# A gather-and-combine expert stage: unrolled, V rows combined in four column groups, accumulator over 128 tokens

## The reference

```python
eid = ...                                   # (C, 128) chosen experts
g = jax.nn.softmax(top_s, axis=-1)...       # (C, 128) gate
u = expert_u[eid]
act = jax.nn.gelu(jnp.einsum('cd,ced->ce', xc, u).astype(jnp.float32))
return jnp.einsum('ce,ced->cd', (g * act).astype(xc.dtype), expert_v[eid])
```

## Time and profile before

| | us |
|---|---|
| median of three runs | 4412.84 |
| span of the profiled execution, first to last instruction (the profile gives no time around it) | 4247.4 |
| PE busy | 3836.9 (90%) |
| DVE busy | 2282.6 (54%) |
| POOL busy | 2122.0 (50%) |
| combine matmuls (L1564), busy | 2040.8 |
| dots (L1762), busy | 1286.0 |
| gathers on POOL, V (L1435) and U (L1426), busy | 1014.6 and 1005.5 |

### The profile page before, as it was taken

The page is one execution under the profiler, slowest core; times in us unless marked ns, Lnnn a source line. Parts: engine busy times, 40 slices in busy tenths (PEclk is TensorE's granted clock), DMA queues, the critical chain, the costliest instruction groups (busy, mean ns, idle before and its releaser), DMA issues.

```text
span 4247.4 us, 40209 instructions
## 1 busy us (share of the span) xinstructions
PE 3836.9 (90%) x10602; PEld 1129.1 (27%) x10602; DVE 2282.6 (54%) x5355; ACT 571.9 (13%) x879; POOL 2122.0 (50%) x2205
## 2 busy tenths in 40 slices
PE   7999998887499999999989989998898999899998
PEld 4444553343122122112212211221121122112111
DVE  2351552242857447655754764575467557546751
ACT  2331552232000001000100100000010000000000
POOL 0000000024356765765666567566657756765674
PEclk9998879998599999999999999999999999999999
DMA  2111006345499999999999999999999999999997
GB/s 69 30 45 42 0 0 193 104 137 175 187 323 366 396 351 327 395 394 323 371 388 360 321 394 390 321 358 384 365 318 385 396 336 350 396 373 318 380 403 259
DMA packets 362556, 1212.93 MB, mean 286 GB/s; under 512 B 42058, under 2 KB 66634, under 8 KB 358748
## 3 DMA queue, kind: packets, MB, share of 16 engines
q0 software_dynamic: 304128, 1107.43, 69.6%
q1 hardware_dynamic: 58204, 102.95, 7.7%
HBM read 1185.97 MB, written 24.26 MB: 285 GB/s over the span
## 4 chain that ended last, share of the span: by engine, by line
PE 33%; issue 16%; DMA 13%; POOL 10%; DVE 4%; ACT 1%; POOLq 0%; DVEq 0%; SPq 0%; ACTq 0%
PE y_acc L1564 21%; DMA v_rows<-expert_v,idx_v 12%; PE qp L1520 6%; POOL v_rows L1435 6%; PE xb L1554 4%; POOL u_rows L1426 4%; DVE x_out L1777 1%; PE tp_r L1541 1%; DMA u_rows<-expert_u,idx_u 0%; PE tp_r L1536 0%; DVE y_out L1783 0%; ACT y_out L1624 0%; DVE u_rows L1762 0%; DMA wq<-w_query 0%; POOLq L1424 0%
## 5 line engine op out<-in xcount | busy, mean ns | idle before, releaser
L1564 PE MATMUL y_acc<-v_rows,w_diag 128*32 128x512 f32 x4224 | 2040.8, 607 | 165.8 <-DMA v_rows<-expert_v,idx_v 63.4
L1762 DVE CUSTOM_DVE_ANT_0 u_rows<-u_rows,xb 128x1024 f32<-128x1024 f32 x1056 | 1286.0, 1220 | 1074.2 <-PE xb L1554 1053.3
L1435 POOL DMA_INDIRECT v_rows<-expert_v,idx_v x1056 | 1014.6, 961 | 707.1 <-PE y_acc L1564 432.2
L1426 POOL DMA_INDIRECT u_rows<-expert_u,idx_u x1056 | 1005.5, 952 | 466.4 <-issue 323.7
L1564 PEld LDWEIGHTS y_acc<-v_rows,w_diag 128*32 128x32 f32 x4224 | 381.7, 110 | 1355.9 <-issue 939.1
L1554 PE MATMUL xb<-parts,pick 96*128 96x512 bf16 x2112 | 654.1, 392 | 60.3 <-DVE dots L1762 37.7
L1554 PEld LDWEIGHTS xb<-parts,pick 96*128 96x128 bf16 x2112 | 147.5, 98 | 833.9 <-DVE dots L1762 593.1
L1520 PE MATMUL qp<-wq,xt 128*128 128x512 f32 x576 | 323.7, 653 | 0.5 <-DMA wq<-w_query 0.5
L352 PE MATMUL zp<-xT,w 128*128 128x512 f32 x512 | 251.4, 619 | 6.1 <-DMA w<-w_in 6.1
L1619 ACT ACTIVATE acts<-dots 128x32 f32<-128x32 f32 x33 | 7.6, 229 | 1662.0 <-DVE dots L1762 1662.0
L1520 PEld LDWEIGHTS qp<-wq,xt 128*128 128x128 f32 x576 | 90.4, 193 | 238.4 <-issue 238.4
(11 more groups left out here) (272 smaller groups left out, 2665.4 us busy)
## 6 DMA issues: line engine op xcount, KB each, us to landing
u_rows<-expert_u,idx_u POOLq DMA_INDIRECT x1056, 6.8
v_rows<-expert_v,idx_v POOLq DMA_INDIRECT x1056, 6.6
w<-w_in SPq DMA_DIRECT2D x16, 512.0 KB, 3.8
xT<-cache_k SPq DMA_DIRECT2D x8, 1024.0 KB, 5.4
xT<-cache_v SPq DMA_DIRECT2D x8, 1024.0 KB, 5.5
wq<-w_query SPq DMA_DIRECT2D x4, 2048.0 KB, 18.5
parts<-x_parts SPq DMA_DIRECT2D x99, 64.0 KB, 6.0
ko<-cache_k SPq DMA_DIRECT2D x8, 768.0 KB, 8.0
```

The lines of the kernel that those rows point to most:

```text
L1426: nc.gpsimd.indirect_dma_start(u_rows[:, t % U_SLOTS, :], None, expert_u, bass.IndirectOffsetOnAxis(ap=idx_u[par][:, t:t + 1], axis=0)).th ...
L1435: nc.gpsimd.indirect_dma_start(v_rows[:, t % V_SLOTS, :], None, expert_v, bass.IndirectOffsetOnAxis(ap=idx_v[par][:, t:t + 1], axis=0)).th ...
L1564: last = nc.tensor.matmul(acc[:, half], w_diag[:, par, t, :], v_rows[:, t % V_SLOTS, half], start=(t == 0), stop=(t == TB - 1))
L1762: nc.vector.tensor_tensor_reduce(out=u_rows[:, t % U_SLOTS, :], in0=u_rows[:, t % U_SLOTS, :], in1=xb[:, t % XB_SLOTS, :], scale=1.0, scal ...
```

## The change

It does six things in `expert_stage`; all else stays.

1. The loops over tiles go: each engine's program is written out over all 33 blocks, with waits against constants.
2. Gathers read their indices straight from idxT; the index copies go. POOL waits for a tile's routing (`kept`) itself.
3. `combine` takes two tokens at a time. Token t adds into column group t mod 4 of the array, that is into partitions 32 g to 32 g + 31 of `acc`; the two tokens' matmuls alternate by half. It waits for both V rows, and frees both slots at its end.
4. `acc` holds 128 tokens. The stationary operand is a window of 32 columns into a zeroed buffer that holds each weight in a place of its own (column 24 + 32 t + t // 4); the window's place decides the row. `weigh` is one strided product.
5. `finish`, `norm`, `store` and `load_resid` come once per tile, on 128 partitions (four transfers of every fourth row each), no longer once per block. The store of a tile is issued behind the second block of the next tile.
6. 6 U slots and 8 V slots, from 8 and 4.

The core of the diff:

```diff
-U_SLOTS = 8
-V_SLOTS = 4
+U_SLOTS = 6
+V_SLOTS = 8
+GROUPS_PE = 4
+EDGE = 24
...
-        w_diag = sb("w_diag", [P, 2, TB, TB])
+        w_diag = sb("w_diag", [P, 2, (TB + 1) * TB])
...
-            with pool.Fori(0, PT) as tile:
-                for j in range(QB):
-                    for t in range(TB):
-                        gather_u(QB * tile + j + 1, t, (j + 1) % 2)
-                        gather_v(QB * tile + j, t, j % 2)
+            for s in range(NTOK + TB):
+                if s < NTOK:
+                    gather_u(s)
+                if s >= TB:
+                    gather_v(s - TB)
...
+            for b in range(NB):
+                r, j = divmod(b, QB)
...
                 sp.wait_ge(dot_done, TB * (b + 1))
+                if b + 2 < NB:
+                    load_parts(b + 2)
+                if (j == 1 and r > 0) or b == NB - 1:
+                    store(r - 1)
+                    load_resid(r)
...
+            def combine(s):
+                b, t = divmod(s, TB)
+                r, j = divmod(b, QB)
+                end = QB - 1 if r < PT else 0
                 if t == 0:
                     pe.wait_ge(w_ready, b + 1)
-                    pe.wait_ge(acc_read, b + 1)
-                pe.wait_ge(v_landed[t % V_SLOTS], 16 * (V_USES * b + t // V_SLOTS + 1))
+                    if j == 0 and r > 0:
+                        pe.wait_ge(acc_read, r)
+                for s2 in (s, s + 1):
+                    pe.wait_ge(v_landed[s2 % V_SLOTS], 16 * (s2 // V_SLOTS + 1))
                 for half in HALVES:
-                    last = nc.tensor.matmul(acc[:, half], w_diag[:, par, t, :], v_rows[:, t % V_SLOTS, half],
-                                            start=(t == 0), stop=(t == TB - 1))
-                last.then_inc(v_free, 1)
+                    for t2 in (t, t + 1):
+                        g, col = t2 % GROUPS_PE, TB * t2 + EDGE - TB // GROUPS_PE * j
+                        last = nc.tensor.matmul(acc[TB * g:TB * (g + 1), half], w_diag[:, b % 2, col:col + TB],
+                                                v_rows[:, (TB * b + t2) % V_SLOTS, half],
+                                                start=(j == 0 and t2 < GROUPS_PE),
+                                                stop=(j == end and t2 >= TB - GROUPS_PE))
+                last.then_inc(v_free, 2)
...
+            for s in range(0, NTOK, 2):
+                for s2 in (s + TB, s + TB + 1):
+                    if s2 < NTOK:
+                        broadcast(s2)
+                combine(s)
+                for s2 in (s, s + 1):
+                    route(s2 // P + 1, s2 % P)
...
+                if b >= 2:
+                    dve.wait_ge(v_free, TB * (b - 1))
+                nc.vector.tensor_tensor(diagonal(b), by_group(acts[:]), by_group(gateT[:, b * TB:(b + 1) * TB]),
                                         ALU.mult).then_inc(w_ready, 1)
...
+            for b in range(NB):
+                r, j = divmod(b, QB)
+                for t in range(TB):
+                    if b + 1 < NB:
+                        dot(TB * (b + 1) + t)
+                    route(r + 1, TB * j + t)
+                if b + 1 < NB:
+                    if (b + 1) % QB == 0:
+                        dve.wait_ge(kept, (b + 1) // QB + 1)
+                    weigh(b + 1)
+                if j == QB - 1 or b == NB - 1:
+                    finish(r)
```

More of the change, by code:

```diff
@@ L1318 @@
 QB = P // TB
-U_SLOTS = 8
-V_SLOTS = 4
+NB = NTOK // TB
+U_SLOTS = 6
+V_SLOTS = 8
 XB_SLOTS = 2
@@ L1480, in _ @@
             load_tokens(1)
-            def block_done(b, j, rows):
-                sp.wait_ge(dot_done, TB * (b + 1))
[L1484 to L1499, removed]
+            for b in range(NB):
+                r, j = divmod(b, QB)
+                if j == 2 and r + 2 <= PT:
+                    sp.wait_ge(xt_used, r + 2)
+                    load_tokens(r + 2)
+                sp.wait_ge(dot_done, TB * (b + 1))
+                if b + 2 < NB:
[3 more added lines that the diff above has]
+                    load_resid(r)
+            store(PT)
+            sp.wait_ge(out_landed, 16 * GROUPS_PE * (PT + 1))
         @block.tensor
@@ L1546, in route, with broadcast @@
                     nc.tensor.transpose(tp[:, 1, :], number[:, 2, :], c.ident[:]).then_inc(turned, 1)
-            def broadcast(b, t, par, loads):
+            def broadcast(s):
+                b, t = divmod(s, TB)
                 if t == 0:
-                    pe.wait_ge(parts_landed[par], 48 * loads)
-                if not isinstance(b, int) or TB * b + t >= XB_SLOTS:
-                    pe.wait_ge(dot_done, TB * b + t - XB_SLOTS + 1)
+                    pe.wait_ge(parts_landed[b % 2], 48 * (b // 2 + 1))
+                if s >= XB_SLOTS:
+                    pe.wait_ge(dot_done, s - XB_SLOTS + 1)
@@ L1553, in broadcast @@
                 for half in HALVES:
-                    last = nc.tensor.matmul(xb[:, t % XB_SLOTS, half], pick[:, t, :], parts[:, par, half],
+                    last = nc.tensor.matmul(xb[:, s % XB_SLOTS, half], pick[:, t, :], parts[:, b % 2, half],
                                             start=True, stop=True)
                 last.then_inc(xb_ready, 1)
-            def combine(b, t, par):
+            def combine(s):
+                b, t = divmod(s, TB)
+                r, j = divmod(b, QB)
+                end = QB - 1 if r < PT else 0
@@ L1572, in _ @@
                 route(0, i)
-            pe.wait_ge(const_ready, 6)
-            for t in range(TB):
-                broadcast(0, t, 0, 1)
-            with pe.Fori(0, PT) as tile:
-                for j in range(QB):
-                    b = QB * tile + j
-                    for t in range(TB):
-                        broadcast(b + 1, t, (j + 1) % 2, 2 * tile + (j + 1) // 2 + 1)
-                        combine(b, t, j % 2)
-                        route(tile + 1, TB * j + t)
-            for t in range(TB):
-                combine(NB - 1, t, 0)
+            pe.wait_ge(const_ready, 5)
+            for s in range(0, TB, 2):
+                broadcast(s)
+                broadcast(s + 1)
+            for s in range(0, NTOK, 2):
[5 more added lines that the diff above has]
+                    route(s2 // P + 1, s2 % P)
         @block.scalar
@@ L1633, in _ @@
             gelu(0)
-            with act.Fori(0, PT) as tile:
-                for j in range(QB):
-                    for t in range(TB):
-                        route(tile + 1, TB * j + t)
-                    gelu(QB * tile + j + 1)
-                    norm(QB * tile + j)
-            norm(NB - 1)
+            for b in range(NB):
[3 more added lines that the diff above has]
+                if b + 1 < NB:
+                    gelu(b + 1)
+                if j == QB - 1 or b == NB - 1:
+                    norm(r)
         @block.vector
@@ L1759, in dot @@
[L1759 to L1761 removed]
+            def dot(s):
+                t = s % TB
+                dve.wait_ge(u_landed[s % U_SLOTS], 16 * (s // U_SLOTS + 1))
+                dve.wait_ge(xb_ready, s + 1)
                 nc.vector.tensor_tensor_reduce(
[L1763 removed]
+                    out=u_rows[:, s % U_SLOTS, :], in0=u_rows[:, s % U_SLOTS, :], in1=xb[:, s % XB_SLOTS, :],
```

187 lines of the change are left out of this document (79 added, 108 removed).

## The result

The kernel after took **4294 us** (median of four runs, 4274 to 4314) against 4416 us for the kernel before beside it: ratio **0.972**, interval 0.968 to 0.976. The forecast was 4100 us with a range of 4045 to 4275. The sign was right and the size was not: 2.8% gained of 7.2% forecast.

A forecast was written before the change was run, and what follows sets the result against it. Transfers at 409 GB/s were taken as the bound nearly throughout: 340 us a tile from 376.9, eight tiles -295 us, tail -20, prologue +2, span 3934 us, plus 165.4 us gives 4100 us; range 4045 to 4275.

The forecast's parts named there:

- the term of 327.7 us a tile: Expert stage: a tile's U and V gathers at 409 GB/s, 128 tokens x 2.56 us, the floor of a tile.
- 3 for routing and 3 for the tile's end: Expert stage: us a tile above the transfers, 3 for PE's routing excess and 3 for the tile's end (between 0 and 8).
- The 165.4 us: Whole kernel: time by which the median run lay above the profiled span, added unchanged to the 3934 us span forecast.
- Combining by pairs: PE's combine: neighbours in different column groups overlap in order, 2.29 us a pair; a routing pair 5.27 us, 2.64 a token.
- the second row comes one gather, 1.28 us, after the first, and the U slots cover that: PE's wait for both V rows of a pair: the delay to later broadcasts and DVE is hidden by U slots.
- Accumulator and unrolling: Block ends and loop turns: DVE away only 1 to 2 us at three of four block ends; the 5.6 us turn goes.
- The tail: Behind the last dot to the span's end: 59 us instead of 78.6, a gain of 20 us.
- Slots: U and V buffers: six U slots cover 15.4 us of transfers, eight V slots double V's cover; 3 us lost at tile end.
- Rival 1: PE's combine: column groups don't overlap, routing tokens take 3.25 us, a tile 362 us; 4274 us, chance 0.17.
- Rival 2: PE's clock: idle time in quiet stretches drops it to half, PE needs about 3.1 us a token; 4290 or 4200 us, chance 0.07.
- Rival 3: Transfers: the mean is the limit, 409 GB/s is paid back later, tile stays at 377 us; 4393 us, chance 0.03.
- Rival 4: PE's combine: changing column group stalls PE, 0.3 us each, a tile 400 us; slower, 4578 us, chance 0.06.

The follow-up runs named there:

- e4: Kernel after with light consumers: broadcast and combine on 64 of 512 columns per half, dot on 64 of 1024; all gathers, waits, slots kept; 4211 us, ratio 0.9531.
- e6: Kernel after with 8 U and 6 V slots instead of 6 and 8; 4187 us, ratio 0.9478 to the kernel before.
- e3: Kernel after with 4 U and 4 V slots instead of 6 and 8; 4459 us, ratio 1.0105 to the kernel before.
- e5: Kernel after with light consumers (64 of 512 columns per half, dot on 64 of 1024) and 4 U and 4 V slots; 4208 us, ratio 0.9525.
- e12: Kernel after unchanged (6 U, 8 V slots), run once more beside three others on one chip; 4320 us, ratio 0.9768 to the kernel before.
- e15: Kernel after with 8 U and 6 V slots, run once more on one chip beside the unchanged kernel after; 4211 us, ratio 0.9512 to the kernel before.
- e2: Kernel after with the pair's two loops exchanged, each token's two halves together; 4291 us, ratio 0.9717 to the kernel before.
- e11: Kernel after with 8 U and 6 V slots and tokens combined one at a time, broadcast between them; 4290 us, ratio 0.9702 to the kernel before.
- e1: Kernel after with the old slots, 8 U and 4 V; 4428 us, ratio 1.0023 to the kernel before.
- e16: Kernel after with the old 8 U and 4 V slots and tokens combined one at a time; 4310 us, ratio 0.9742 to the kernel before.
- e9: Kernel after (6 U, 8 V slots) with each V gather issued two tokens earlier in POOL's order; 4224 us, ratio 0.9546 to the kernel before.
- e13: Kernel after with 6 U and 6 V slots, on one chip beside the unchanged kernel after; 4228 us, ratio 0.9549 to the kernel before.
- e14: Kernel after, buffers unchanged, but V gathers wait until at most six V rows are held or under way; 4227 us, ratio 0.9541 to the kernel before.

## Why the prediction was right or wrong

**The step that failed: "At 409 GB/s a gather takes 0.524 / 409 = 1.28 us", and with it the term of 327.7 us a tile.** The 60 us that it came from are real, and the kernel after has such stretches too (409 to 411 GB/s at 2600 to 2612). But a row that stood in the earlier trace rows spoke against it as the rate of the stage. The gathers' queue took 69.6% of 4247.4 us on each engine, 2956 us, for 2,112 gathers: 1.40 us a gather, 375 GB/s while busy. That row alone could still put the difference down to routing; the runs after it can't. The same product gives 1.39 in the kernel after (68.5% of 4293.8), in e4 (69.7% of 4206.3) and in e6 (70.5% of 4178.4). It was never below that, and with four V slots the consumers raise it: 1.45 in e3 against 1.40 in e5, which has the same slots. 256 x 1.393 is 357 us a tile, 29 us over the term. The other 17 us of the 46 that a tile missed are mostly idle time of the DMA engines: a share of 0.946 of 386.4 us leaves 21 us, where the forecast had 3 for routing and 3 for the tile's end. The slots set it: in e6 a share of 0.983 of 371.8 us leaves 6, and the tile is 14.6 us shorter. On one chip, e12 and e15, it is 388.4 against 373.8.

**The base.** The 165.4 us that the prediction added to the span were a difference between executions: 1.8 us lie there. This error went the other way and hid nearly half of the first: the span was forecast at 3934 us and came out 360 us longer, and the forecast time missed by only 194. That is luck. 3934 us plus 8 x 46.4 is 4305, and the span came out at 4293.8; most of the 11 us left are the prologue (first dot at 1114.6 us instead of 1121.4, with 2 us allowed for more). With the tile of e6, 371.8 us, the same sum gives 3934 + 254 = 4188 us for the span; e6's is 4178.4, with a first dot 18 us earlier than the sum allows (1105.4) and a tail 9 us longer (67.9). So, with these two against each other, the terms besides the gathers and the idle time were about right.

**Combining by pairs** was sized at 5.27 us for a routing pair and measured 4.61: the full overlap, the lower bound of its combine term. The step that took 2.29 us for a combine pair held the matmuls to their order; 1.85 us came (1597.96 to 1599.81), and as much in the other order (e2). The Trainium skill (TensorEngine Tiling (Array Packing), Key Properties) has tiles of the array work in parallel, and the trace agrees, with 1.91 us for eight matmuls. Combining by pairs is worth 2.0 to 2.4% with 8 and 6 slots (e11 against e15 and e6), and it costs 2.9% with 8 and 4 (e1 against e16). The words "the second row comes one gather, 1.28 us, after the first, and the U slots cover that" left out that the pair also holds two V slots; with four, that is half of V's cover.

**Accumulator and unrolling** were right in kind and undersized, 13.3 us a tile (e16) instead of about 10. **The tail** was right: 58.7 us for 59.

**Slots.** "Six U slots are 6 x 2.56 = 15.4 us of transfers" and "Eight V slots double the cover where V waits now" both failed as cover. The step counted a slot's mean time; in the kernel after DVE waited up to 10.7 us for one late row, and POOL, with nothing else to stop it, stood until that row's dot was done.

**The rivals.** Rival 1 gives nearly the measured time (4274 us) and is wrong as a mechanism: the groups overlap. Rival 2 is half there: the granted clock fell to 0.83 over the stage, to 0.80 in the quiet stretch (between the levels of 1.2 and 2.4 GHz), but e6 moves 369 GB/s at 0.85, and e4 364 at 0.58, so it isn't what held the kernel back. Rival 3, at 0.03, came nearest: the mean is the limit. That 409 GB/s is paid back in the next stretch is seen at 2600 to 2616 us and not shown beyond. Its time, 4393 us, kept the tile at 377 us on a base that was 164 us too high. The Trainium skill (DMA: Bandwidth & Descriptors, Specifications) gives a core about 358 GB/s of HBM, half of a stack's 716; the stage held 364 to 369 in e4 to e6, a little above that and far from 409. No run shows that HBM is what limits it. Rival 4 did not happen: in the pair at 1593.35 us the matmuls of one group start 0.43 to 0.45 us apart, as they did before.

## What to carry to other kernels

Take a transfer rate from the whole stage, best from a queue's share of the span divided by its transfers, never from the fastest stretch; and take the base from the execution whose time is to be predicted, not from a profile of another one. When a change makes a wait cover several buffers at once, count the buffers that it holds. Where one engine issues two streams in turn, ask at which wait it will stand: the faster runs here were those in which it stood often and briefly ahead of V, and not long behind the last U slot. Depths are to be tried downwards too, and so is the order of issue (e9).

## What was not expected

Two V slots more cost 2.2% (e12 against e13 and e14), though the eighth is never filled; with V issued two tokens earlier all eight are filled and cost nothing (e9). A U row's gather can end long after later ones are mostly done: DVE waited 8.64 us with the DMA engines full. The Trainium skill (DMA: Bandwidth & Descriptors, Why a DMA increments its semaphore by 16 and not by 1) says that the engines of one transfer finish independently and that only the last of them tells that the data has landed; the count above, 5.2 gathers that the mean engine has finished beyond the awaited one, agrees.

A packet of 4 KB takes 159 ns at the median in the kernels before and after and in e4, but 172 to 174 ns in the mean: some 3% take over 250 ns. In the first profile of the kernel before they lie where PE routes (7 to 9% of the packets there in steps of 40 us, mostly under 3% elsewhere), in the kernel after and in e4 they are spread over the stage. The first gather of the stage, with nothing under way, has them too: mostly 170 to 1100 ns for its first 30 packets, 159 for nearly all behind them. Whether an engine that has run dry is what makes them slow, and so what lies between 409 and 375 GB/s, stays open.
